# Router and one-hot choice with their weights stationary, queries rotated as halves, first loads on one queue

## What is computed

```python
p_group = softmax(h @ w_rg + b_rg)              # router: 4 groups
g_idx, g_prob = argmax(p_group), max(p_group)
e_logits = (h @ w_re + b_re).reshape(..., 4, 4) # router: 16 experts
top_logits, top_idx = top_k(e_logits[g_idx], 2)
y = sum over e of gates[e] * ((silu(h @ w_gate[e]) * (h @ w_up[e])) @ w_down[e])
# second block, both layers, 16 query heads of 64:
q = concat(q1 * cos - q2 * sin, q2 * cos + q1 * sin, rest)   # the first 16 of 64 features turned
```

## Time and profile before

| what | us |
|---|---|
| three runs, median (lowest to highest) | 2655.25 (2654.47 to 2656.56) |
| the profiled execution | 2660.26 |
| its span, first to last instruction | 2658.5 |
| PE busy in it | 2560.8 (96%) |
| DVE busy | 1278.0 (48%) |
| ACT busy | 1086.6 (41%) |
| POOL busy | 884.9 (33%) |
| mean granted clock of PE | 0.982 of full speed |

### The profile page before, as it was taken

One profiled execution on the slowest core, in us unless ns is written; L12 is line 12 of the kernel. 1 busy time (PEld: TensorE's weight loads), 2 busy tenths in 40 slices (PEclk: granted clock), 3 DMA queues, 4 the chain that ended last, 5 costly groups with the idle time before them and its releaser, 6 DMA issues.

```text
span 2658.5 us, 30601 instructions
## 1 busy us (share of the span) xinstructions
PE 2560.8 (96%) x12190; PEld 2072.3 (78%) x12190; DVE 1278.0 (48%) x1823; ACT 1086.6 (41%) x1696; POOL 884.9 (33%) x390
## 2 busy tenths in 40 slices
PE   8988999999899999999999999999999999999997
PEld 6767787888766788878788888766888878788886
DVE  2994357778467458453511010576367353610113
ACT  3354225667337456333322122357374233322221
POOL 3471000000231344432344344321444431344344
PEclk9998989999999999999999999999999999999999
DMA  6332338999421233332233333211333332233232
GB/s 211 88 92 60 105 131 309 351 383 372 140 77 35 80 96 101 113 106 69 70 99 117 95 95 103 73 48 48 95 96 101 113 103 64 79 95 119 88 95 79
DMA packets 220077, 318.80 MB, mean 120 GB/s; under 512 B 17184, under 2 KB 176032, under 8 KB 219808
## 3 DMA queue, kind: packets, MB, share of 16 engines
q1 hardware_dynamic: 201184, 284.24, 33.0%
q10 hardware_dynamic: 16592, 24.72, 2.7%
q0 software_dynamic: 2160, 7.89, 0.8%
HBM read 301.06 MB, written 15.75 MB: 119 GB/s over the span
## 4 chain that ended last, share of the span: by engine, by line
PE 88%; DVE 9%; ACT 1%; DMA 1%; issue 1%; DVEq 0%; ACTq 0%; POOL 0%
PE ps L670 81%; PE ps L685 4%; PE ps L835 3%; DVE stats L2133 1%; DVE rows L2143 1%; DVE ix L2246 1%; DVE top L2244 1%; DVE pair_l L2420 0%; ACT pair_h L1730 0%; DVE rows L2155 0%; DMA rows<-in_x 0%; DMA ysum<-ys,slot_no 0%; DVE qf L2511 0%; DVE mv L2136 0%; DVE vbuf L2509 0%
## 5 line engine op out<-in xcount | busy, mean ns | idle before, releaser
L611 POOL TENSOR_TENSOR w_lo<-w_raw,w_hi 128x1024 fp32r<-128x1024 f32 x331 | 812.8, 2465 | 1402.7 <-ACT w_hi L1492 1402.7
L670 PE MATMUL ps<-x_hi,w_hi 128*128 128x512 f32 x1624 | 647.6, 399 | 3.7 <-DVE x_lo L2050 2.7
L670 PE MATMUL ps<-x_hi,w_lo 128*128 128x512 f32 x1624 | 634.3, 391 | 0.0
L670 PE MATMUL ps<-x_lo,w_hi 128*128 128x512 f32 x1624 | 633.7, 390 | 0.0
L1492 ACT ACTIVATE w_hi<-w_raw 128x1024 fp32r<-128x1024 f32 x331 | 341.3, 1052 | 499.7 <-PE ps L670 480.8
L670 PEld LDWEIGHTS ps<-x_hi,w_hi 128*128 128x128 f32 x1624 | 305.7, 188 | 88.0 <-issue 21.3
L670 PEld LDWEIGHTS ps<-x_lo,w_hi 128*128 128x128 f32 x1624 | 306.0, 188 | 64.9
L670 PEld LDWEIGHTS ps<-x_hi,w_lo 128*128 128x128 f32 x1624 | 306.1, 188 | 62.9 <-issue 2.9
L2656 DVE TENSOR_TENSOR fhd<-fsg,ps 128x512 f32<-128x512 f32 x44 | 30.2, 688 | 383.0 <-PE ps L670 382.9
L2420 DVE TENSOR_TENSOR pair_l<-pair_raw,pair_h 128x2048 fp32r<-128x2048 f32 x84 | 189.8, 2288 | 35.1 <-ACT pair_h L1730 35.0
L1730 ACT ACTIVATE pair_h<-pair_raw 128x2048 fp32r<-128x2048 f32 x84 | 157.9, 1911 | 4.2 <-ACT yb L1745 2.8
(11 more groups left out here) (403 smaller groups left out, 4321.3 us busy)
## 6 DMA issues: line engine op xcount, KB each, us to landing
w_raw<-in_w_in SPq DMA_DIRECT2D x102, 512.0 KB, 3.7
w_raw<-in_ffn_wi SPq DMA_DIRECT2D x88, 512.0 KB, 3.5
pair_raw<-in_w_gate SPq DMA_DIRECT2D x56, 512.0 KB, 6.3
pair_raw<-in_w_up SPq DMA_DIRECT2D x56, 512.0 KB, 7.7
pair_raw<-in_w_down SPq DMA_DIRECT2D x56, 512.0 KB, 7.0
w_raw<-in_ffn_wo SPq DMA_DIRECT2D x44, 512.0 KB, 3.6
w_raw<-in_w_out SPq DMA_DIRECT2D x24, 512.0 KB, 3.6
kv_raw<-in_ckv_w SPq DMA_DIRECT2D x20, 512.0 KB, 3.9
```

The source lines that it names most:

```text
L611: pool.tensor_tensor(w_lo[:, slot, :], w_raw[:, slot, :], w_hi[:, slot, :].bitcast(F32), ALU.subtract).then_inc(lo_done, 1)
L670: ins = pe.matmul(o, a, b, start=first, stop=last)
```

## The change

- First loads: x's two halves are issued by SP after slab 0 and before slabs 1 and 2. ACT splits one slab, not two, ahead of the high parts of x.
- Router: `route_w` (20 columns) is the stationary operand and `xt` moves 512 columns, eight products in all. ACT copies the 20x512 result to `route_f`, four transposes bring it back to token rows. The wait for four parts of `xt` goes. Five of the eight steps of `kv(20)` stand ahead of the count, the rest behind it. Two of the four bias additions move behind `group_hot` on DVE.
- First block: `sel` is the stationary operand and the rows `res` move in two halves of 512 columns. ACT copies the two halves to `xblk`, and PE transposes them as it does for the later blocks.
- Rotations of queries: ACT takes another copy of each query, `q_hi` (fp32r), before `qf`, from product 6 on after waiting for an earlier rotation; DVE subtracts to get `q_lo` (`low_query`); PE adds two fp32r products with `rot_r`, a copy of `rot2`. Five calls of `flush` per layer go.

The diff without its lists of semaphores and counters (a line of three points marks what is left out):

```diff
@@ -268,6 +268,7 @@
...
     route_w = place("route_w", [P, KD, 20], F32, 86)
+    route_f = place("route_f", [20, T], F32, 64)
...
@@ -325,6 +326,10 @@
...
+
+    q_hi = place("q_hi", [P, 4, T], F32R, 82)
+    q_lo = [place(f"q_lo{i}", [P, T], F32R, at) for i, at in enumerate((18, 20, 44, 46))]
+    rot_r = place("rot_r", [P, P], F32R, 91)
...
@@ -517,7 +522,13 @@
...
+            x = A["x"][0].rearrange("(t p) d -> p t d", p=P)
             for n, src in enumerate(slabs_first()):
+
+                if n == 1:
+                    for h in range(2):
+                        sync.dma_start(res[:, :, 512 * h:512 * h + 512], x[:, :, 512 * h:512 * h + 512])\
+                            .then_inc(x_landed[h], 16)
                 if n == N_IN - RING:
...
@@ -1079,19 +1090,24 @@
...
             normed_to_features()
-            pe.wait_ge(s["hi_ready"], NT)
             for k in range(KD):
                 pe.wait_ge(s["hi_ready"], k + 1)
-                for t in range(NT):
-                    mm(ps[:, t, 0:20], xt[:, k, t * P:t * P + P], route_w[:, k, :], k == 0, k == KD - 1,
-                       "narrow_products" if k == KD - 1 and t == NT - 1 else None)
-
-            kv(20)
+                mm(ps[0:20, 0, :], route_w[:, k, :], xt[:, k, :], k == 0, k == KD - 1,
+                   "narrow_products" if k == KD - 1 else None)
+            pe.wait_ge(s["narrow_copied"], 1)
+            for t in range(NT):
+                flip(ps[:, 1, t * P:t * P + 20], route_f[:, t * P:t * P + P], "narrow_products" if t == NT - 1 else None)
+
+            beside = kv_steps(20)
+            for _ in range(5):
+                next(beside)
             pe.wait_ge(s["group_hot"], 1)
...
             mm(ps[:, 6, 16:20], consts["one"], total[:, 0, :], inc="counted")
+            for _ in beside:
+                pass
             kv(21)
...
@@ -1103,10 +1119,12 @@
...
                 pe.wait_ge(s["chosen"], 1)
-                for k in range(KD):
+                for half in range(2):
                     for t in range(NT):
-                        mm(block_bank(k), of_chunk(res[:, t, :], k), sel[:, t, :], t == 0, t == NT - 1,
-                           "block_turned" if k == KD - 1 and t == NT - 1 else None)
+                        mm(ps[:, 2 + half, :], sel[:, t, :], res[:, t, 512 * half:512 * half + 512], t == 0, t == NT - 1,
+                           "first_rows" if t == NT - 1 else None)
+                pe.wait_ge(s["first_block"], 2)
+                turn_rows(0)
...
@@ -1118,6 +1136,9 @@
...
                 pe.wait_ge(s["block_lo"], b)
+                turn_rows(b)
+
+            def turn_rows(b):
                 for k in range(KD):
...
@@ -1221,7 +1242,12 @@
...
                 def turn_query(c):
-                    turn(4 + c, 6 if c in (1, 3) else 7, qf[:, c, :], 3 + c)
+                    bank = small(4 + c, 6 if c in (1, 3) else 7)
+                    pe.wait_ge(s["query_lo"], done.at("query_lo", c + 1))
+                    if l == 0 and c == 0:
+                        pe.wait_ge(rot_ready, 1)
+                    mm(bank, rot_r[:, :], q_hi[:, c % 4, :], True, False)
+                    mm(bank, rot_r[:, :], q_lo[c % 4][:, :], False, True, inc="small_products")
...
@@ -1238,12 +1264,10 @@
...
                 pair_f((0, 1), x_hi, x_lo)
-                flush()
                 turn_query(1)
...
                 pair_f((2, 3), x_hi, x_lo)
-                flush()
                 turn_query(3)
...
@@ -1596,13 +1619,9 @@
             act.dma_start(const[:, 0:P], A["tables"][:, 0:P]).then_inc(first_landed, 16)
-            x = A["x"][0].rearrange("(t p) d -> p t d", p=P)
-            for h in range(2):
-                act.dma_start(res[:, :, 512 * h:512 * h + 512], x[:, :, 512 * h:512 * h + 512]).then_inc(x_landed[h], 16)
-
-            split(2)
+            split(1)
             high_parts(x_hi)
-            split(RING - 2)
+            split(RING - 1)
             act.dma_start(const[:, P:NCONST], A["tables"][:, P:NCONST]).then_inc(start, 16)
...
@@ -1747,11 +1766,17 @@
...
+            act.wait_ge(s["narrow_products"], 1)
+            act.activation(route_f[:, :], ps[0:20, 0, :], ACT.Copy).then_inc(s["narrow_copied"], 1)
             pair_high(0)
...
             kv_store(10)
+            for half in range(2):
+                act.wait_ge(s["first_rows"], half + 1)
+                act.activation(xblk[:, 0, 512 * half:512 * half + 512], ps[:, 2 + half, :], ACT.Copy)\
+                   .then_inc(s["first_block"], 1)
             act.wait_ge(s["gate_in"], 2)
...
@@ -1789,6 +1814,7 @@
...
+            act.activation(rot_r[:, :], consts["rot2"], ACT.Copy).then_inc(rot_ready, 1)
             for l in range(LAYERS):
...
@@ -1815,10 +1841,14 @@
...
                     dst = qf[:, j - 2, :] if j >= 2 else (kr[:, :] if j == 0 else vr[:, :])
+                    if j >= 6:
+                        act.wait_ge(s["small_products"], done.at("small_products", j - 2))
+                    if j >= 2:
+                        act.activation(q_hi[:, (j - 2) % 4, :], ps[:, (j % 6), :], ACT.Copy).then_inc(s["query_hi"], 1)
                     act.activation(dst, ps[:, (j % 6), :], ACT.Copy).then_inc(s["evacuated"], 1)
...
                         split(1 if j == 1 else 2)
-                done.passed(products=10)
+                done.passed(products=10, small_products=11)
                 units = len(UNITS2)
...
@@ -2353,13 +2383,15 @@
...
             link(ins)
-            for t in range(NT):
-                ins = dve.tensor_tensor(res[:, t, :], res[:, t, :], gain[:, 1, :], ALU.add)
-            link(ins)
-
-
-            dve.wait_ge(s["narrow_products"], 1)
-            link(dve.tensor_tensor(rt[:, :, 0:20], ps[:, 0:NT, 0:20],
+
+            def add_bias(tiles):
+                for t in tiles:
+                    ins = dve.tensor_tensor(res[:, t, :], res[:, t, :], gain[:, 1, :], ALU.add)
+                link(ins)
+
+            add_bias((0, 1))
+            dve.wait_ge(s["narrow_products"], 2)
+            link(dve.tensor_tensor(rt[:, :, 0:20], ps[:, 1, :].rearrange("p (t n) -> p t n", t=NT)[:, :, 0:20],
                                    route_b[:, :].unsqueeze(1).broadcast_to([P, NT, 20]), ALU.add))
...
@@ -2385,6 +2417,7 @@
...
             dve.tensor_tensor(total, before[:, NT - 1, :], g_hot[:, NT - 1, :], ALU.add).then_inc(s["group_hot"], 1)
+            add_bias((2, 3))
...
@@ -2515,6 +2548,13 @@
...
+                def low_query(c):
+
+                    dve.wait_ge(s["query_hi"], done.at("query_hi", c + 1))
+                    dve.wait_ge(s["evacuated"], done.at("evacuated", c + 3))
+                    dve.tensor_tensor(q_lo[c % 4][:, :], qf[:, c, :], q_hi[:, c % 4, :].bitcast(F32), ALU.subtract)\
+                       .then_inc(s["query_lo"], 1)
+
...
@@ -2522,11 +2562,20 @@
...
                    .then_inc(s["banks_read"], 1)
+                low_query(0)
+                low_query(1)
                 dve.wait_ge(s["small_products"], done.at("small_products", 3))
...
                 dve.tensor_copy(ks[upper, 0, :], ps[upper, 6, :]).then_inc(s["banks_read"], 1)
-                for c in range(5):
-                    turn_query(c)
+                turn_query(0)
+                low_query(2)
+                low_query(3)
+                turn_query(1)
+                turn_query(2)
+                low_query(4)
+                low_query(5)
+                turn_query(3)
+                turn_query(4)
...
@@ -2568,11 +2617,13 @@
...
                         divide(u - 1)
+                    if u in (1, 2):
+                        low_query(5 + u)
                     if u in (3, 5, 7):
...
                         low_part((u - 5) // NT)
-                done.passed(small_products=11, banks_read=11, turned=9, scores=n, probs_t=n, scores_read=n, probs=2 * n,
+                done.passed(small_products=11, banks_read=11, turned=9, query_hi=8, scores=n, probs_t=n, scores_read=n, probs=2 * n,
                             sums_inverted=n, hi_ready=8, values=n, products=10 + 8)
...
```

More of the change, by code:

```diff
@@ L92 @@
     "chunk_ready",
-    "small_products", "turned",
+    "small_products", "turned", "query_hi", "query_lo",
     "scores", "scores_read", "maxima",
@@ L111 @@
     "first_half_summed",
-    "group_hot", "counted", "chosen", "slots_ready", "first_gates", "first_gates_copied",
+    "group_hot", "counted", "chosen", "first_rows", "first_block", "slots_ready", "first_gates", "first_gates_copied",
     "both_full", "silu_unit", "hidden_unit", "hidden_turned", "hidden_h", "hidden_l", "down_done",
@@ L411, in build @@
         out_normalised, out_scaled, out_ready = sem("out_normalised"), sem("out_scaled"), [sem(f"out_ready{t}") for t in range(NT)]
-        blanked, tapped, cleared, scattered, block_stored, gathered = sem("blanked"), sem("tapped"), sem("cleared"), sem("scattered"), sem("block_stored"), sem("gathered")
```

(3 more changed lines are left out.)

## The result

The changed kernel took a median of 2636.82 us in four runs (2634.96 to 2637.73), the kernel before 2655.9 in its four beside them. The ratio is 0.9922, with a 95% interval of 0.9896 to 0.9948: 19.1 us faster where the forecast said 21.9, and 2636.8 where it said 2633.4. The two profiled executions differ by more, 2660.26 against 2634.96, which is 25.3; where the extra 6 us are is part of the question.

The account below looks back on a forecast made before the run. PE bounds the kernel, with 88% of the chain (DVE 9%). Gains of 2.5 + 12.8 + 6.8 - 0.2 = 21.9 us give 2638.4 for the profiled execution and 2633.4 for the median (0.60), range 2625 to 2646.

Parts of the forecast that it names:

- First loads: Start of kernel: x's first half lands near 6.9 us instead of 9.27; gain 2.5 us, between 0 and 3.6.
- Router: Last transpose of x to the experts' first product: turned products and choice gain 12.8 us, bounds 0 and 14.5.
- Rotations: Query rotations in two layers: 2 x (1.7 + 1.0 + 0.7) = 6.8 us gained, less 0.2 for the rot_r copy.
- a verdict on the whole edit, worth 0: Rival at x's loads: one queue puts nothing first, first transpose stays at 9.27; 2635.9 us, chance 0.15.
- Slab 1's slack: After x's transposes: slab 1's low part comes some 4.1 us after the last, PE wants it at 5.2; holds by 1.1.
- the profile's 5 us over the median: Whole kernel: profiled execution 2660.26 us, median 2655.25, 5.0 less; the difference was carried over to the forecast.
- Rival 2: Router and choice: clock stays at 1.2 GHz from 366 to the choice's end, router gains nothing; 2646.2 us, chance 0.10.
- the 1.9 us of a dip inside the choice: Router and choice: if the clock falls again only for a while, as in the first window loop, it costs 1.9 us.
- the window loop, +0.7 by count: Each layer's window loop: three rotations save 1.2 us on PE, DVE gets later; gain 0.7, bounds -0.5 and 1.2.
- Rival 3: Both layers' rotations: DVE decides, contested low parts eat what PE spares, gain 0; 2640.2 us, chance 0.12.
- Rival 4's ring: Rotations: waits circle through ACT, POOL, PE and DVE, eight waits late, 24.8 us lost; 2665 us, chance 0.03.
- Drains: Flushes before rotations: only two of five a layer drain anything, 0.5 us each; six of ten aren't there.

Follow-up runs that it names:

- the second trace: Changed kernel with the old router and old choice put back, bias additions and count where they were: 2648.23 us, ratio 0.9970 to the kernel before.

## Why the prediction was right, and where not

**First loads: mechanism right, the landing put 0.6 us too early.** 1.96 us for 2.5 in this pair of traces, 1.9 to 2.6 against the median trace. The step that failed is the landing of x's first half, put at 6.9 from the bytes in all by 9.2 us and found at 7.51 (7.33 to 7.78 in ten traces). The sum counted only x's own bytes and those issued ahead of it, 1.64 MB, but by 7.5 us 1.94 MB had begun to move (258 GB/s over that time). The version with x first shows the same: 1.12 MB were needed, and by 6.1 us it was 1.42 (232 GB/s). So some 0.3 MB of what is issued behind x has begun to move before x's half has landed. The Trainium skill's section that stood against this part ("DMA: Bandwidth & Descriptors", "Issuing engines are not separate DMA queues") is borne out: x on ACT's own queue lands at the same 7.48 if slabs 1 and 2 are held back, so the choice of queue by itself is worth nothing. The prediction read it as a verdict on the whole edit, worth 0. But the edit also put x ahead of two slabs, of which that section says nothing, and this is what gained. Slab 1's slack came as forecast: its low part ends at 17.9, 4.1 us after the last transpose.

**Router: every step within 0.8 us, but the base was one execution, and one price was wrong.** From the last transpose: logits 8.2 (forecast 8.5), group choice 11.2 (11.5), last sel 18.1 (18.5), choice done 25.3 (25.5), experts 30.05 (30.85). Against the profiled execution the gain is 13.7 for 12.8. But the kernel without this part is 11.4 slower by the medians. The term mis-sized is the 13.28 us of the earlier trace rows together with the 17 us of half clock of the earlier trace rows: I took them as the old router's fixed cost and then carried the profile's 5 us over the median as if they lay elsewhere. The same code took 10.3 in the second trace. And the sum let the turned products gain 6.3 us by fewer and longer passes (13.28 to 6.9): at full clock they gain none. That 12.8 came near the 13.7 of the two traces does not prove that price: both are taken from the same execution of the kernel before, half clock included. Rival 2 (half clock in the new products) did not come in the changed kernel's trace, nor the 1.9 us of a dip inside the choice.

**Rotations: right up to the wait, wrong behind it.** 0.80, 2.13 and 2.75 for 0.91, 2.2 and 2.7, with rotation 4 contested instead of 3 and POOL 1 us later behind ACT's wait, as written. The failed step is the window loop, +0.7 by count, -0.6 in the trace. Its bound of -0.5 was near. Two subtractions in DVE's first rounds push its later rounds back, and PE goes from no wait to 1.6 us of waits, more than the 1.2 that three rotations spare. That they are the cause is shown as far as the version without them shows it: the waits go, in both layers, and 0.8 us behind the second scores come back, though ACT's copies and wait went with them. So 2.1 a layer, 4.3 in all, and some 1 us a layer by a clock dip that mostly went away; the medians say 5.5 for 6.6, so the total is nearer than its mechanism. Why the dip went is not shown; the version with two old rotations has it in one of its two layers. Rival 3 falls at zero gain, though its engine is the one that ate part of it. Rival 4's ring did not form; the one sign of it is the wait of 0.83 for w_lo.

**Drains: as forecast,** four of ten, 0.5 each.

**The sum.** The parts undone one by one cost 1.8 + 11.4 + 5.5 = 18.7; the whole is 19.1. With some 4 us of interval on each of them that shows no interaction, but can't exclude one of several us. At full clock they are 2.0 + 5.3 + 4.3 = 11.6 us by the traces; the other 7 or so are then half clock that no longer happens, most of it in the old router. The forecast of 21.9 counted the half clock of one execution as work that goes away; that it came near 19.1 is in part luck. The half clock is also why the two profiles differ by 25: summed over the span, but for the last 12 or 13 us, which are at half clock in every trace, the kernel before lacked 41.0 us of clock, the changed one 20.5, part of both in pauses. Other traces with the new router lack 22 to 32, and the one with the old router put back 29, so one trace's sum says little; the mean clocks of all runs say more.

## What to carry over

Price a stretch of small matmuls at both clock levels before you turn it: here 64 passes of 20 columns cost as much as 16 of 512 at full clock (7.0 to 7.1 us, estimates, against 7.04), and 5 to 9 us more as they ran, with what stood behind them; 64 passes of 128 columns cost 15.5 us at full clock, and there turning them gained 6.0. An operation added to another engine is free only up to that engine's next deadline: count its rounds in the loop where it lands, not only its mean share. And put what is wanted first ahead in the order of issue, until the next thing behind it becomes late.

## What the runs showed of the hardware

- The granted clock fell 2.1 us into a pause of PE of 4.2 us, and came back 4.6 us into products of 512 columns. In the kernel before it fell at 366.4, 2.2 us after the last transpose and while the 20-column products ran, and stayed low 17 us; in the second trace of the same code it fell 5.4 us after the last transpose and stayed low 10 us. A fall is worth 1.7 to 8.5 us of missing clock in these traces. Every trace has three before 255 us, one between 296 and 316, one within 1.3 us of the experts' first product, and the last 12 to 13 us at half clock; the places of the others differ from one trace to the next.
- While POOL subtracts from SBUF, DVE's operations with all operands in SBUF end only when its instruction does or up to 0.55 us later: 2.45 to 2.79 us for 0.69, 2.56 and 1.52 for a scaling of 0.35, and 2.25 for a copy of two elements a partition that takes 0.17. A multiply that reads PSUM (0.69 at 754.43, beside POOL from 754.55) is not held. The Trainium skill, "SBUF — State Buffer", section "Who interferes with whom", says so of operations with two SBUF inputs and of scalings and copies, and calls the port pair an exclusive lock; the rows agree. That a copy of 128x2 elements is held for 2.25 us I had not expected.
